# One head's copy per round behind the maxima, the ninth query product in the values' bank, and the query turns behind the exponentials, in the first attention of a two-block kernel

## What is computed

```python
qkv = h @ w_in
q = rmsnorm_2(q.reshape(B, S, A_HEADS, A_HEAD_DIM), q_gain)
k = rmsnorm_2(k.reshape(B, S, A_KV_HEADS, A_HEAD_DIM), k_gain)
scores = einsum(q, k) * scale + bias          # over a block of 128 and the one before it
m = max(max(scores), sink)
p = exp(scores - m)
probs = p / (sum(p) + exp(sink - m))
o = einsum(probs, v)
return o @ w_out
```

## Time and profile before

| what | us |
|---|---|
| median of 3 runs | 2663.81 (2663.8, 2663.81, 2667.22) |
| the profiled execution's own time | 2663.84 |
| its span in the trace | 2662.6 |
| PE busy | 2635.7 |
| DVE busy | 1436.4 |
| ACT busy | 989.9 |
| POOL busy | 319.5 |

### The profile page before, as it was taken

The page is one execution under the profiler, slowest core; times in us unless marked ns, Lnnn a source line. Parts: engine busy times, 40 slices in busy tenths (PEclk is TensorE's granted clock), DMA queues, the critical chain, the costliest instruction groups (busy, mean ns, idle before and its releaser), DMA issues.

```text
span 2662.6 us, 31241 instructions
## 1 busy us (share of the span) xinstructions
PE 2635.7 (99%) x12738; PEld 2210.8 (83%) x12752; DVE 1436.4 (54%) x2266; ACT 989.9 (37%) x1650; POOL 319.5 (12%) x388
## 2 busy tenths in 40 slices
PE   9999999999999999999999999999999999999999
PEld 8898888888887788789988888888888788888887
DVE  7637547574757444356774343453434676543433
ACT  4344334342444222236642222322222586422221
POOL 0000010000021000015530000100000586200000
PEclk9999999999999999999999999999999999999999
DMA  5322325523223445464323332233232101233222
GB/s 161 119 88 90 101 80 177 167 80 111 79 95 95 107 103 103 94 112 104 107 95 106 96 100 87 87 111 95 95 95 78 62 22 38 91 110 96 95 91 68
DMA packets 278438, 258.92 MB, mean 97 GB/s; under 512 B 40324, under 2 KB 270743, under 8 KB 278295
## 3 DMA queue, kind: packets, MB, share of 16 engines
q1 hardware_dynamic: 278279, 256.93, 32.4%
q10 hardware_dynamic: 16, 0.00, 0.0%
HBM read 242.23 MB, written 14.68 MB: 96 GB/s over the span
## 4 chain that ended last, share of the span: by engine, by line
PE 90%; DVE 3%; ACT 3%; issue 2%; POOL 2%; DMA 0%; SPq 0%; POOLq 0%; DVEq 0%; ACTq 0%
PE bank L1183 29%; PE bank L1185 29%; PE bank L1184 29%; PE bank L1345 1%; POOL Wl L2489 1%; DVE Wl L1924 1%; ACT Wh L1557 0%; ACT Z L1847 0%; POOL TMP L2496 0%; PE bank L1409 0%; DVE Pl L2444 0%; PE bank L1282 0%; PE bank L1505 0%; DMA Z<-bias_scratch 0%; ACT Hh L1837 0%
## 5 line engine op out<-in xcount | busy, mean ns | idle before, releaser
L1183 PE MATMUL bank<-Hh,Wl 128*128 128x512 f32 x2136 | 838.4, 393 | 2.2 <-DVE Hl L1943 1.8
L1185 PE MATMUL bank<-Hh,Wh 128*128 128x512 f32 x2136 | 831.8, 389 | 0.0
L1184 PE MATMUL bank<-Hl,Wh 128*128 128x512 f32 x2136 | 831.5, 389 | 0.0
L1924 DVE TENSOR_TENSOR Wl<-RAW,Wh 128x1024 fp32r<-128x1024 f32 (+2 forms) x420 | 493.6, 1219 | 161.8 <-ACT Wh L1557 161.1
L1557 ACT ACTIVATE Wh<-RAW 128x1024 fp32r<-128x1024 f32 (+2 forms) x454 | 441.1, 1022 | 365.9 <-PE bank L1185 341.7
L1183 PEld LDWEIGHTS bank<-Hh,Wl 128*128 128x128 f32 x2136 | 401.1, 188 | 87.9 <-DVE Hl L1943 3.1
L1184 PEld LDWEIGHTS bank<-Hl,Wh 128*128 128x128 f32 x2136 | 401.1, 188 | 84.0 <-issue 1.7
L1185 PEld LDWEIGHTS bank<-Hh,Wh 128*128 128x128 f32 x2136 | 401.0, 188 | 83.8
L1183 PE MATMUL bank<-Ph,Wl 128*128 128x512 f32 x1152 | 452.0, 392 | 0.8 <-DVE Wl L1924 0.5
L1185 PE MATMUL bank<-Ph,Wh 128*128 128x512 f32 x1152 | 448.7, 389 | 0.0
L1184 PE MATMUL bank<-Pl,Wh 128*128 128x512 f32 x1152 | 448.3, 389 | 0.0
(11 more groups left out here) (336 smaller groups left out, 2501.1 us busy)
## 6 DMA issues: line engine op xcount, KB each, us to landing
RAW<-in_ffn_wg SPq DMA_DIRECT2D x44, 1024.0 KB, 5.3
RAW<-in_ffn_wu SPq DMA_DIRECT2D x44, 1024.0 KB, 5.3
RAW<-in_ffn_wd SPq DMA_DIRECT2D x32, 1024.0 KB, 5.1
RAW<-in_w_up SPq DMA_DIRECT2D x22, 1024.0 KB, 5.1
RAW<-in_w_in SPq DMA_DIRECT2D x20, 1024.0 KB, 5.2
RAW<-in_ffn_wd SPq DMA_DIRECT2D x16, 768.0 KB, 4.4
bias_scratch<-M SPq DMA_DIRECT2D x16, 512.0 KB, 8.2
RAW<-in_w_down SPq DMA_DIRECT2D x8, 1024.0 KB, 5.1
```

Source lines behind the costliest of these rows:

```text
L1183: mm(o, ll, rh, start=start, stop=False)
L1184: mm(o, lh, rl, start=False, stop=False)
L1185: return mm(o, lh, rh, start=False, stop=stop)
L1924: tt(Wl[:, n % 3, x:y], RAW[:, n % 2, x:y], f(Wh[:, n % 3, x:y]), ALU.subtract).then_inc(*w_lo.up(*([("w_lo", n)] if i else [])))
```

## The change

`attend_a_order` is given `split` and `load`. Four things move in the list:

1. `q_out(6 + i)` of a round goes from ahead of the scores to behind `a_soft(i)`, and one is in each round: u = 6 moves from round 1 to round 0. u = 5 stays ahead of the scores of round 0.
2. The query product of round 1 (u = 8, the ninth) takes its bank from `summed` and no longer from `products[0]`.
3. `next_tile` splits nothing ahead at u = 8; the split of tile `("aq", 3)` and the load that went with it come at the end of round 1, behind `a_exp(1)` and `a_norm(1)`.
4. `q_turn(g)` in rounds 2, 6 and 10 goes from ahead of the round's query product to behind `a_exp(i)` and `a_norm(i)`, which is also behind `values(i - 3)`, and ahead of `attended`.

```diff
     def q_product(u, ring=None):
         g, b = u // 4, u % 4
         if b == 0:
-            tile[g] = next_tile("aq", g, 1)
+            tile[g] = next_tile("aq", g, 0 if g == 2 else 1)
...
     for i in range(16 + LV):
-        for u in {0: (5,), 1: (6, 7)}.get(i, (6 + i,) if i < 10 else ()):
-            q_out(u)
+        if i == 0:
+            q_out(5)
         if i == 10:
             banks.join(products[0])
         if i < 16:
...
                 scored.take(("a_s", i, m))
             do("a_scores", i)
             do("a_soft", i)
+            if i < 10:
+                q_out(6 + i)
             if i == 1:
                 do("a_k_low", 1)
             if i + 2 < 16:
...
             turns(i - LT)
         if i in (1, 5, 9):
             do("a_q_norm", i // 4 + 1)
-        if i % 4 == 2 and i < 11:
-            q_turn(i // 4 + 1)
         if i < 9:
-            q_product(7 + i)
+            q_product(7 + i, summed if i == 1 else None)
         if i >= LV:
             values(i - LV)
         if i < 16:
             do("a_exp", i)
             do("a_norm", i)
+        if i % 4 == 2 and i < 11:
+            q_turn(i // 4 + 1)
+        if i == 1:
+            split()
+            load()
         if i >= LV and (i - LV) % 2:
             attended((i - LV) // 2)
```

More of the change, by code:

```diff
@@ L667, in order @@
     now["low"] = "pool"
-    attend_a_order(steps, banks, tmps, next_tile, norm_step, hkeys, pv, xv, h_new, h_pair, stats, add_x, do, dense)
+    attend_a_order(steps, banks, tmps, next_tile, split, load, norm_step, hkeys, pv, xv, h_new, h_pair, stats, add_x, do, dense)
     now["low"] = "dve"
@@ L710, in out_partial, with attend_a_order @@
     return run
-def attend_a_order(steps, banks, tmps, next_tile, norm_step, hkeys, pv, xv, h_new, h_pair, stats, add_x, do, dense):
+def attend_a_order(steps, banks, tmps, next_tile, split, load, norm_step, hkeys, pv, xv, h_new, h_pair, stats, add_x, do, dense):
     do("a_begin")
```

## The result

The changed kernel takes 2673.41 us (median of 7 runs, 2673.19 to 2675.8), the kernel before, measured beside it, 2666.28 us (7 runs, 2663.8 to 2667.22). So it is slower by about 8 us, 0.3%. The prediction had 2670.0, in a range of 2664 to 2674.5, with 0.60 on slower. The direction and the wide range held. The forecast's own narrower range, 2668.9 to 2671, was missed, and so was the size: +6.2 was forecast.

What follows compares the result with a forecast made beforehand. The prediction took PE as the bound, with about 4 us of waits to give. Its terms -0.25 + 1.1 + 2.07 + 3.25 summed to +6.2 us, 2670.0 us, own range 2668.9 to 2671, whole range 2664 to 2674.5.

Steps and rivals of the forecast that it cites:

- What bounds the kernel: Rounds: PE is the bound after rounds 1 to 3; the stage has about 4 us of waits to give.
- Rounds 1 to 3: Three PE waits, 3.6 us, go; u = 10 then waits for ACT's copy of u = 9: -0.25 us left.
- The split and its load: Tile ("aq", 3): later load delays head 4's bias copies and maxima, so u = 12 starts later: +1.1 us.
- Rival (d): Head 4's bias copies overtake the load and land in 2.7 us: -1.1, 2668.9 us; chance 0.07.
- The turn of group 2: Rounds 6 and 7: PE waits 2.35 us ahead of u = 14 where it waited 0.28: +2.07 us.
- Group 3: Rounds 9 and 10: later sums of u = 15 and turn delay round 10's last output product: +3.25 us.
- The clock: Rounds: no clock term in the sum; the clock had stayed full through all waits of the rounds so far.
- Rival (a): New waits in rounds 3, 7 and 10 bring one fall of PE's clock, 3.4 us: 2673.4 us; chance 0.23.
- two falls of the clock: Two falls of PE's clock, or a wait overlooked: slower, chance 0.03; two falls set the range's upper end.
- Rival (b): Second attention: the clock fall at 2129 does not come, 3.4 us come back: 2666.6 us; chance 0.13.
- Rival (c): Rounds 1 to 3: the three waits go, nothing takes their place: -3.6, 2660.2 us; chance 0.14.
- Reference for the sum: The sum was made against the profiled execution's own 2663.84 us, 0.03 above the median.

Runs made afterwards that it cites:

- e1: The changed kernel with its group turns put back ahead of the query product in rounds 2, 6 and 10: 2666.83 us, ratio 1.0008.
- e6: The kernel before with u = 8's new bank, the later split and load, and the copy of u = 9 ahead of head 2's exponentials: 2664.05 us.
- e8: As e7, but with the load ahead of head 4's bias copies, as in the change: 2664.28 us, ratio 0.9998.
- e7: The kernel before with u = 8's new bank, later split, load behind head 4's bias copies, earlier u = 9 copy, only group 1's turn moved: 2662.86 us.
- e12: The kernel before with only the turn of group 2 (round 6) moved behind the exponentials: 2668.68 us, ratio 1.0014.
- e2: The kernel before with only the group turns moved behind the exponentials: 2669.67 us, ratio 1.0018.
- e4: The kernel before with only the copies q_out(6) to q_out(15) moved behind the maxima, one a round: 2667.39 us, ratio 1.0010.
- e3: The changed kernel with products of no use in two PE waits, 20 ahead of u = 10, 24 between round 10's output products: 2669.32 us.
- e10: The changed kernel with only the 20 products of no use ahead of u = 10 in round 3: 2671.08 us, ratio 1.0023.
- e11: The changed kernel with only the 24 products of no use between the output products of round 10: 2671.76 us, ratio 1.0022.
- e5: The kernel before with only u = 8's new bank and the split and load behind the norm of head 1: 2664.46 us, ratio 0.9999.
- third group: The last four follow-up kernels, on one chip with their own runs of the kernel before, whose median was 2664.82 us.

## Why the prediction was right and wrong

**What bounds the kernel: right.** Only PE's own work and some 4 us of waits were there to be had, and the most that any version got of it is 3.74 us at u = 10.

**Rounds 1 to 3: right.** The three waits went and the copy of u = 9 took their place, behind the group's copies on ACT. u = 10 came at -0.47 against the forecast -0.25, by a single wait of 2.95 us in place of three.

**The split and its load: mis-sized.** The order on SP was right: in e1 the last bias copy goes out 2.14 us later against the stage's start. The landing was not. It took about 5 us there against 6.4 before, the maxima came 0.7 us later and not 2.2, and the product they might have held up did not wait. The term is 0 and not +1.1 at that point; where PE is earlier (e6, e8) it is real, 1.3 us between e7 and e8 in the rounds. Rival (d) did not happen either: copies with no load ahead of them landed in 2.7 us.

**The turn of group 2: right.** +2.07 forecast, +2.12 in the changed kernel, +2.10 alone in e12. The wait lies in two places, for head 5's norm and for the copy, as the text had it.

**Group 3: right.** +3.25 forecast, +3.1 measured, split as forecast. By the starts in the traces the turn alone (e2) costs 1.83 us between the scores of head 8 and the last output product of round 10, where 1.75 were forecast, and the late sums alone (e4) 1.49 for 1.5.

**The clock: the step that failed.** The sum took PE's clock as full, a term of zero, because it had stayed full through all waits of the rounds so far. The terms for the waits came out well: +6.2 forecast, +5.1 without the term of the bias copies, against 4.7 in the trace and 4.45 by the time of e3. What was missing is half clock behind the new waits: 6.7 us in the profiled execution, 3.8 by the median, 4.0 given back by the fills of e3. The waits that had left the clock full were of 1.7 us and less, and the new ones are longer. Each of the waits of 2.94 to 3.20 us that no fill covered, two in each of the two traces of the changed kernel and one each in e10 and e11, had a stretch at half clock behind it. Those between 1.9 and 2.4, or split in two, had it in some traces and not in others: the 2.35, 2.22 and 1.94 of e2 with one, the 2.22 of e12 and the 2.1 to 2.2 of round 2 in e1, e5 and e6 without.

Rival (a) had this mechanism, at 0.23, but as one fall of 3.4 us. In the traces there are three falls of 1.5 to 2.7 us, so by their number it is the case of "two falls of the clock", which had 0.03. That the time came out at (a)'s 2673.4 is luck: several smaller falls on top of a sum of waits that was 1.5 us too high. The price of one fall was 0.75 to 2.7 us over all traces. It depends on how long the half clock lasts, and what of it lies in the wait itself costs nothing.

The Trainium skill, page "TensorE: Matmul & The Clock Gate", section "HAM oscillation — how this bites in real kernels", describes a kernel in which a wait for data behind every tile lets TensorE fall to half clock each time. The rows here agree, with waits for ACT, POOL and DVE in place of a DMA (granted 0.50 behind each of the three). The same section of the Trainium skill counts half of the throttled time as the loss. Here the missing share of the clock in the four stretches of 20 us after is 0.17 + 0.03 + 0.05 + 0.17, or 8.4 us, which is the loss that this way of counting would give, an estimate. 6.7 us of it reached the end of the rounds, and of the fall at 2130 in the kernel before nothing did, so the measured loss can be well under it.

**Rival (b): did not happen, and wrong in its price.** In the changed kernel the fall is still there, behind the same wait, at 2142 (2.59 us). And (b) gave 3.4 us for a fall that costs nothing in that place. In e12 and e10 the clock was full behind that wait with everything before it moved, and no time came back; but in both it had fallen some 20 us earlier, so the clean case is e5.

**Rival (c): nearly there, and not by this order.** e7 reaches its u = 10 (-3.74 against -3.6), but needs the copy of u = 9 ahead of the turn and the turns of the other groups where they were.

**Reference for the sum.** The own execution, 2663.84, is at the low end of the runs of before; with more of them the kernel before shows times near 2664.4 and near 2667 (in the third group 16 and 11 runs). What makes the difference between these two, no trace shows. Against the 2664.82 of the third group the forecast sum of +6.2 stands beside +8.5.

## What to carry to other kernels

Price a wait on a saturated TensorE twice: by its length, and by the clock behind it. Three waits of 0.5 to 1.7 us, 3.6 in all, left the clock full in rounds 1 to 3 here; one of 2.95 in their place did not. Where such a wait can't be avoided, products of no use into a bank that is free are worth a try: 44 of them gave back 4 us here. They don't give back the waits: e3 is still 4.45 us over the kernel before.

A step moved in a shared list moves in every queue. The turn of a group behind the exponentials cost 0.7 us by u = 10, 2.1 in round 7 and 1.8 in round 10 (e2, e12): its copies on ACT or its low parts on DVE came later and held up a bank that PE wanted next. Move a step only in the round that needs it.

Before a fall of the clock, or any slower engine, is priced, see whether the engine waits behind it: at 2130 us half of the clock was free of charge, at 1250 it cost 1.3 to 2.7 us.

## What was unexpected of the hardware

PE's clock can be at half for several microseconds with no effect on the time (12.80 against 12.82 us over the same instructions). The same wait is not always followed by a fall: the two waits of round 7, 0.7 and 1.3 us, had one behind them in both traces of the changed kernel (1280 to 1300 us at a granted 0.95 in the first), and none in e3, e10 and e11, in which they were as long. And a fall can come with no wait ahead of it, as between 2110 and 2115 us in e12. So the time of one kernel varies with the clock: e2 from 2666.92 to 2672.58, with the granted clock falling from 0.999 to 0.996 as the time rises. And the same four bias copies behind the same load took up to 6.4 us to land in the kernel before and up to 5.5 in e1.
